# Attention heads: key norms as a product with ones over all partitions, and the inverse root as exponential of a logarithm

## The reference, cut to what matters

```python
def _rms(x, g):
    y = x * lax.rsqrt(jnp.mean(x * x, axis=-1, keepdims=True) + 1e-6)
    return y * g

k = jnp.concatenate([k_nope, jnp.broadcast_to(k_rope[:, :, None, :], ...)], axis=-1)
q, k = _rms(q, q_norm_g), _rms(k, k_norm_g)          # then rope on the last 64 channels of each
s = jnp.einsum('bhqd,bhkd->bhqk', q, k) * 192 ** -0.5
o = jnp.einsum('bhqk,bhkd->bhqd', jax.nn.softmax(s, axis=-1), v)
```

## Time and profile before

| | |
|---|---|
| median of three timed runs | 1948.47 us (1947.96 to 1952.48) |
| span of the profiled execution, first to last instruction | 1945.0 us |
| its own time | not listed apart; the median is 3.5 us above the span |
| TensorE, VectorE, ScalarE, GpSimd busy | 98%, 72%, 36%, 47% of the span |
| mean granted TensorE clock | 0.995 of full |

### The profile page before, as it was taken

One profiled execution on the slowest core, in us unless ns is written; L12 is line 12 of the kernel. 1 busy time (PEld: TensorE's weight loads), 2 busy tenths in 40 slices (PEclk: granted clock), 3 DMA queues, 4 the chain that ended last, 5 costly groups with the idle time before them and its releaser, 6 DMA issues.

```text
span 1945.0 us, 24388 instructions
## 1 busy us (share of the span) xinstructions
PE 1901.5 (98%) x9095; PEld 1580.3 (81%) x9095; DVE 1394.2 (72%) x1433; ACT 703.6 (36%) x966; POOL 909.7 (47%) x634
## 2 busy tenths in 40 slices
PE   7999999999999999999999999999999999999998
PEld 6788888778888888888888788878787878888877
DVE  7989988566449898989888774754723756666583
ACT  5433344421243333333331200342321245565543
POOL 6866666533235555555655556323133513212442
PEclk9999999999999999999999999999999999999999
DMA  5122234455112232322264434111141310000052
GB/s 167 44 63 67 87 109 141 147 163 156 44 43 87 66 97 65 97 75 86 82 242 147 146 103 168 55 33 33 33 133 52 89 37 1 12 12 1 1 173 65
DMA packets 190890, 166.42 MB, mean 86 GB/s; under 512 B 11267, under 2 KB 168912, under 8 KB 190800
## 3 DMA queue, kind: packets, MB, share of 16 engines
q1 hardware_dynamic: 189520, 162.82, 26.4%
q10 hardware_dynamic: 1280, 2.35, 0.4%
HBM read 134.73 MB, written 30.41 MB: 85 GB/s over the span
## 4 chain that ended last, share of the span: by engine, by line
PE 81%; DVE 11%; issue 3%; ACT 2%; POOL 2%; DMA 1%; SPq 0%; ACTq 0%; DVEq 0%; POOLq 0%
PE ps L953 32%; PE ps L1250 19%; PE ps L1100 15%; PE ps L1665 2%; PE ps L1483 2%; PE ps L1516 1%; PE ps L1518 1%; PE ps L1517 1%; PE ps L1497 1%; PE ps L1494 1%; PE ps L1500 1%; PE ps L1491 1%; PE ps L1503 1%; DVE win_a L2942 1%; DVE prob L2990 1%
## 5 line engine op out<-in xcount | busy, mean ns | idle before, releaser
L824 POOL TENSOR_TENSOR small<-ones 128x1 f32<-128x1 f32 x76 | 26.3, 346 | 501.4 <-PE ps L953 432.8
L953 PE MATMUL ps<-xb_hi,whi 128*128 128x512 f32 x752 | 247.2, 396 | 7.0 <-DVE xb_lo L2898 1.9
L953 PE MATMUL ps<-xb_hi,wlo 128*128 128x512 f32 x752 | 244.1, 392 | 0.0
L953 PE MATMUL ps<-xb_lo,whi 128*128 128x512 f32 x752 | 243.8, 392 | 0.0
L829 POOL TENSOR_TENSOR wlo<-raw,whi 128x1024 fp32r<-128x1024 f32 (+1 forms) x73 | 198.8, 2723 | 6.1
L869 POOL TENSOR_TENSOR wlo<-w_sums,whi 128x512 fp32r<-128x512 f32 x80 | 138.0, 1744 | 82.2 <-ACT whi L1963 82.2
L953 PEld LDWEIGHTS ps<-xb_hi,whi 128*128 128x128 f32 x752 | 141.2, 190 | 40.9 <-issue 5.7
L953 PEld LDWEIGHTS ps<-xb_lo,whi 128*128 128x128 f32 x752 | 142.1, 189 | 30.3 <-issue 0.2
L953 PEld LDWEIGHTS ps<-xb_hi,wlo 128*128 128x128 f32 x752 | 142.1, 189 | 30.2
L2367 DVE SCALAR_TENSOR_TENSOR ps<-glu_pad,tab,ps 128x1024 f32<-128x1024 f32 x116 | 149.2, 1286 | 2.9
L923 POOL TENSOR_SCALAR prob<-prob,small 128x512 f32<-128x512 f32 x64 | 50.7, 806 | 188.2 <-DVE small L2999 188.0
(11 more groups left out here) (489 smaller groups left out, 4855.8 us busy)
## 6 DMA issues: line engine op xcount, KB each, us to landing
t<-in_w_mod SPq DMA_DIRECT2D x48, 256.0 KB, 3.1
f_scratch<-t SPq DMA_DIRECT2D x22, 512.0 KB, 2.7
raw<-in_w_down SPq DMA_DIRECT2D x22, 512.0 KB, 4.4
raw<-in_w_up SPq DMA_DIRECT2D x40, 256.0 KB, 3.7
w_raw<-in_w_up SPq DMA_DIRECT2D x40, 256.0 KB, 3.6
raw<-in_w_in SPq DMA_DIRECT2D x18, 512.0 KB, 4.0
raw<-in_w_in SPq DMA_DIRECT2D x36, 256.0 KB, 3.7
w_in_raw<-in_w_in SPq DMA_DIRECT2D x32, 256.0 KB, 3.7
```

The costliest lines, as they stand in the source:

```text
L824: nc.gpsimd.tensor_tensor(small[:, 106 + slab.slot:107 + slab.slot], ones[:, 0:1], ones[:, 0:1], ALU.mult)
L953: ins = mm(dst[j], w, r[j], start=first and f, stop=last and l)
```

## The change

The rows of inverse roots are made without ever having the keys on the partitions. A matrix of ones as the weights leaves a sum over the partitions on every partition of the result. `KSQ` holds the squares of the rope channels, high halves on partitions 0 to 63 and low halves on 64 to 127 (made once, by ScalarE and VectorE), and the head's own squares go into `rkbc` itself. In each head TensorE adds both in PSUM, in three pieces of 256, 512 and 512 columns (banks 7, 5 and 6), behind `pv` and ahead of V. ScalarE reads the sums, writes the logarithm of the mean to `rkbc`, and then, in place, the exponential of -0.5 times it. A dummy activation ahead of the logarithms and one behind the exponential bring the tables for logarithm and square root.

```diff
-        def key_sums(n):
-            if n == 4:
-                pe.wait_ge(sem("lora_sq"), 4)
-                for t in range(KT):
-                    mm(PS[:, SC + 32 + t:SC + 33 + t], sqkr[:, t * P:(t + 1) * P], ones[0:ROPE, 0:1], start=True, stop=True)
...
-        gemm(j, L, XBh, XBl, KD, w8, between=key_sums)
+        gemm(j, L, XBh, XBl, KD, w8)
...
+        def key_sums(h):
+            if h == 0:
+                pe.wait_ge(sem("ksq_ready"), 2)
+            else:
+                pe.wait_ge(sem("pt_lo"), 6 * 4 * h)
+            for a, b in ((S, NKEY), (0, H), (H, S)):
+                o = PS[:, 5 * H + a:5 * H + b]
+                mm(o, onesr[:, :], KSQ[:, a:b], start=True, stop=False)
+                last = mm(o, ones[:, :], rkbc[:, a:b], start=False, stop=True)
+                if a != 0:
+                    last.then_inc(sem("ksum_pe"), 1)
...
-                query_product(h, c, 0, 0, 4 * c).then_inc(sem("nope_pe"), 1)
+                query_product(h, c, 0, 0).then_inc(sem("nope_pe"), 1)
...
             if h == 0:
                 warm(2)
+            key_sums(h)
...
+                    if i == 3:
+                        pe.wait_ge(sem("k_log"), 2 * h + 2)
...
-            key_scales(h, 0)
             pe.wait_ge(sem("q_fold"), GOES_ON["q_fold"][1] + 2 * h + 1)
+            pe.wait_ge(sem("k_log"), 2 * h + 1)
             scores(g, 0, 0, 512, 0)
-            key_scales(h, 1)
-            key_scales(h, 2)
...
+        act.wait_ge(sem("lora_sq"), 4)
+        fn(KSQ[0:ROPE, :], sqkr[:, :], ACT.Copy).then_inc(sem("ksq_hi"), 1)
...
-                fn(sqk[:, k], PS[:, k], ACT.Square).then_inc(sem("kn_sq"), 1)
+                fn(rkbc[:, k], PS[:, k], ACT.Square).then_inc(sem("kn_sq"), 1)
...
-            act.wait_ge(sem("k_var"), h + 1)
-            fn(ksd, kvar, ACT.Sqrt, scale=1.0 / QH, bias=eps_col).then_inc(sem("k_sd"), 1)
...
+            fn(sd[:, 12:13], ones[:, 0:1], ACT.Ln)
+            for n, (a, b) in enumerate(((S, NKEY), (0, S))):
+                act.wait_ge(sem("ksum_pe"), 2 * h + n + 1)
+                fn(rkbc[:, a:b], PS[:, 5 * H + a:5 * H + b], ACT.Ln, scale=1.0 / QH, bias=eps_col).then_inc(sem("k_log"), 1)
             if h % 2 == 0:
...
+                for i in range(3):
+                    value_hi(i)
+            act.wait_ge(sem("k_log"), 2 * h + 2)
+            fn(rkbc[:, :], rkbc[:, :], ACT.Exp, scale=-0.5).then_inc(sem("k_scale"), 1)
+            if h % 2 == 0:
+                for i in range(3, 5):
+                    value_hi(i)
+            fn(sd[:, 12:13], ones[:, 0:1], ACT.Sqrt)
...
-        link(nc.vector.tensor_copy(krc, PS[:, SC + 32:SC + 32 + KT]))
+        nc.vector.tensor_copy(onesr[:, :], ones[:, :]).then_inc(sem("ksq_ready"), 1)
+        dve.wait_ge(sem("ksq_hi"), 1)
+        tt(KSQ[ROPE:P, :], sqkr[:, :], f32(KSQ[0:ROPE, :]), ALU.subtract).then_inc(sem("ksq_ready"), 1)
...
-            dve.wait_ge(sem("kbc_read"), 3 * h + 3)
+            dve.wait_ge(sem("k_scale"), h + 1)
```

More of the change, by code:

```diff
@@ L284, in build_program @@
     Vl = at("v_lo", [P, KT, 2 * VD], F32R, o_xbh + 43008)
-    sqk = at("sq_head", [P, NKEY], F32, o_xbh + 53248)
+    sqk = at("sq_head", [P, S], F32, o_xbh + 53248)
     qwork = at("q_rope_work", [P, S], F32, o_xbh + 58368)
@@ L288, in build_program @@
     PTh = at("pt_hi", [P, KT, 2 * P], F32R, o_xah)
+    KSQ = at("k_rope_squares", [P, NKEY], F32R, o_t + 20480)
+    onesr = at("ones_r", [P, P], F32R, o_t + 25600)
     rkbc = at("k_scale_bc", [P, NKEY], F32, o_xah + KT * 2 * P * 4)
@@ L1432, in key_product @@
             return last
-        def key_sum(t):
-            return mm(PS[:, SC + 256 + t:SC + 257 + t], sqk[:, t * P:(t + 1) * P], ones[:, 0:1], start=True, stop=True)
+        def key_sums(h):
[9 more added lines that the diff above has]
+                    last.then_inc(sem("ksum_pe"), 1)
         def query_sum(t):
@@ L1442, in query_sum, with query_product @@
                 last.then_inc(sem("qsum_pe"), 1)
[L1444 to L1454, removed]
+        def query_product(h, c, col, at_bank):
             slot = Lin(SLABS["heads"] + h).slot
@@ L1461, in query_product @@
                 mm(o, whi[:, slot, w], CQh[:, k, q], start=k == 0, stop=False)
-                if sums is not None:
-                    key_sum(sums + 2 * k)
                 mm(o, whi[:, slot, w], CQl[:, k, q], start=False, stop=False)
-                if sums is not None:
-                    key_sum(sums + 2 * k + 1)
                 last = mm(o, wlo[:, slot, w], CQh[:, k, q], start=False, stop=k == 1)
-            if sums == 4:
-                key_sum(8)
-                key_sum(9).then_inc(sem("ksum_pe"), 1)
             return last
@@ L1716, in build_program @@
     tot = small[:, 110:126].rearrange("p (s t) -> p s t", s=2)
-    rsum4, krc, kvar, ksd = small[:, 10:14], small[:, 48:58], small[:, 66:76], small[:, 76:86]
+    rsum4 = small[:, 10:14]
     def scalar_program(act):
@@ L2191, in scalar_program, with value_hi @@
             fn(QRs[0:ROPE, :], qwork[0:ROPE, :], ACT.Copy).then_inc(sem("qr_hi"), 1)
-            act.wait_ge(sem("k_var"), h + 1)
-            fn(ksd, kvar, ACT.Sqrt, scale=1.0 / QH, bias=eps_col).then_inc(sem("k_sd"), 1)
             act.wait_ge(sem("qn_lo"), GOES_ON["qn_lo"][1] + 2 * h + 2)
             fn(sqk[:, H:S], PS[:, H:S], ACT.Square).then_inc(sem("qn_sq"), 1)
-            if h % 2 == 0:
[L2197 to L2206, removed]
+            def value_hi(i):
+                act.wait_ge(sem("v_pe"), 5 * (h // 2) + i + 1)
+                fn(Vh[:, 2 * i:2 * i + 2, :], PS[:, H * (2 + i):H * (3 + i)].rearrange("p (t n) -> p t n", t=2),
+                   ACT.Copy).then_inc(sem("v_hi"), 1)
+            fn(sd[:, 12:13], ones[:, 0:1], ACT.Ln)
+            for n, (a, b) in enumerate(((S, NKEY), (0, S))):
+                act.wait_ge(sem("ksum_pe"), 2 * h + n + 1)
+                fn(rkbc[:, a:b], PS[:, 5 * H + a:5 * H + b], ACT.Ln, scale=1.0 / QH, bias=eps_col).then_inc(sem("k_log"), 1)
+            if h % 2 == 0:
+                for i in range(3):
[6 more added lines that the diff above has]
+            fn(sd[:, 12:13], ones[:, 0:1], ACT.Sqrt)
             act.wait_ge(sem("head_var"), h + 1)
@@ L3054, in vector_program @@
                 pool_low(3)
-            dve.wait_ge(sem("ksum_pe"), h + 1)
-            tt(kvar, PS[:, SC + 256:SC + 256 + KT], krc, ALU.add).then_inc(sem("k_var"), 1)
             query_lo(1)
@@ L3060, in vector_program @@
             query_fold(0)
-            dve.wait_ge(sem("k_sd"), h + 1)
-            nc.vector.reciprocal(rcp[:, 0:KT], ksd).then_inc(sem("k_rcp"), 1)
             if h:
```

## The result

The changed kernel takes 1954.47 us, the median of 13 runs (1950.87 to 1956.68), against 1948.52 for the kernel before (13 runs, 1945.47 to 1952.48). The ratio is 1.0028, 95% interval 1.0021 to 1.0036: 4 to 7 us slower, at the edge of what is called no change here. 1951.4 was forecast, with 1945.0 to 1955.5 as its range. The profiled execution has a span of 1953.3, 8.3 more than before.

What follows compares the result with a forecast made beforehand. TensorE, busy in 98% of the span, was taken as the bound. The terms -2.4 - 1.65 + 0.6 + 1.4 + 1.7 + 3.3 = +2.95 us on about 1948.5 gave 1951.4 us, range 1945 to 1955.5.

Steps and rivals of the forecast that it cites:

- Part two: Heads 1 to 3: removing ten key sums gains 0; pv still waits for VectorE's rope query, gap 0.45 to 2.75 us.
- faster rival: Heads 1 to 3: the rotated query comes earlier, 2.3 us won in each, no gaps: 1941.2 us, chance 0.08.
- Parts three and four: New sums cost 3.1 us per head, +0.85 each odd head; logarithm chain +0.6 in head 0, +1.4 in head 2.
- The reserve: Odd heads: ScalarE's logarithms, loads and exponential end 0.65 us before the query's square root wants ScalarE.
- slower rival: ScalarE becomes the bound through table changes in the heads, 7.7 us more: 1959, chance 0.16.
- part one: Ahead of the heads: removing the rope keys' ten one-column sums gains 2.4 us, their low-clock stretch 1.65 more.
- Part five: Low clock behind the gaps in heads 1 to 3: chance 0.6 each, 1.65 us lost each, two likeliest, +3.3.
- hit every time: All three gaps in heads 1 to 3 are followed by a low-clock stretch: 1953.1 us, chance 0.14.
- the cases: Number of gaps followed by low clock: none or one 0.20, two 0.42, all 0.14; 1948.2 to 1953.1 us.
- The base: Kernel before: about 1948.5 us, profiled span 1945.0 plus 3.5 us taken as lying around the span.

Runs made afterwards that it cites:

- two_more_loads: The changed kernel with a dummy logarithm and a dummy root more in heads 1 and 3, so two table loads more in each: 1958.85 us, ratio 1.0043.
- wide_fill3: The changed kernel with three warming products of 512 columns, read by nobody, filling the whole gap ahead of pv in heads 1 to 3: 1950.48 us.
- sums_in_gap: The changed kernel with the new key sums moved from behind pv into the gap ahead of it in heads 1 to 3: 1940.74 us, ratio 0.9966.
- ga_sums_back: The changed kernel with the ten one-column products on the rope keys' squares back in the first ga projection, read by nobody: 1955.22 us.
- narrow_fill: The changed kernel with ten one-column products, read by nobody, in the gap ahead of pv in heads 1 to 3: 1954.03 us.
- wide_fill: The changed kernel with two warming products of 512 columns, read by nobody, in the gap ahead of pv in heads 1 to 3: 1954.10 us.

## Why the prediction was right, and where it was not

The measured time lies in the range, and parts two to four held in their mechanism. But the change is 6.0 us by the medians where 2.95 was forecast: the clock cost more than forecast in both of its terms, in parts one and five.

*Part two held.* VectorE's rope query stays where it was, and the removed sums became wait. Its first step and the one that `pv` waits for, in head 3 of the changed kernel:

```profile
1789.14 1.23 DVE L3035 TENSOR_TENSOR q_rope_work<-ps,cos_sin_q 64x1024 f32<-64x1024 f32 x1 [0.55 <-ACT q_rope_work L2159]
...
1792.80 1.21 DVE L3042 TENSOR_TENSOR q_rope_work<-ps,q_rope_work 64x1024 f32<-64x1024 f32 x1
```

`pv` starts 4.92 us behind the first step, as before (1785.14 to 1790.05, 4.91). The gap is 2.56 where 2.75 was forecast. The faster rival falls with it.

*Parts three and four held, each a little dear.* The sums take 1798.98 to 1801.31 and 0.4 for the slower first product behind, 2.7 us instead of 3.1. Without the longer `pv`, head 3 lost 0.6 us from `pv` to the scores row (5.8 - 4.0 - 1.25), against 0.85, and head 1 lost 0.4. The even heads came close: head 0 lost 0.5 (from -1.2 to -0.7 in the table) against 0.6, and head 2 lost 1.3 (2.8 - 1.5) against 1.4. ScalarE in head 3:

```profile
1801.91 1.12 ACT L2187 ACTIVATE k_scale_bc<-ps,small 128x1024 f32<-128x1024 f32 x1 [1.71 <-PE ps L1438]
1803.04 1.28 ACT L2192 ACT_TABLE_LOAD   x1
1804.34 1.27 ACT L2192 ACTIVATE k_scale_bc<-k_scale_bc 128x1280 f32<-128x1280 f32 x1
1805.63 1.28 ACT L2196 ACT_TABLE_LOAD   x1
...
1807.46 0.21 ACT L2198 ACTIVATE small<-small 128x8 f32<-128x8 f32 x1 [0.34 <-DVE small L3065]
```

The logarithm at 1.1 and the exponential at 1.27 are as taken, and each load is followed within 0.02 us. The reserve is 0.34 us, half of the forecast's 0.65, and it holds. So the slower rival did not come. The drain of 1.38 us that the Trainium skill gives (ScalarE: Activation LUTs, What ACT_TABLE_LOAD costs) shows in neither kernel, and two_more_loads, which would have lost about 10 us by it, lost 4.4. In head 0 the wait for the logarithm is 2.4 (2.25 was forecast), and the one for the fold follows, as worked out; the wait for `v_lo`, 2.0 before, is still there with 0.8. In head 2 TensorE waits for the fold (0.8) and not for the logarithm, as said.

*The step that failed is the clock's in part one.* "Both the sums and this stretch go" is wrong in its second half: the sums went (2.4 us in the trace), the stretch stands behind the next block of one-column products. Of the nine traces, the two with both blocks have one stretch there, behind the first; of the seven with one block, six have one behind it. Removing a block saved its time and no stretch, so the term of -1.65 was 0.

*Part five was mis-sized.* Three gaps of three were followed by 0.50, not two: the rival "hit every time". `pv` took 5.17, 5.16 and 4.92 us where 3.67 is its price, so a stretch there cost 1.25 to 1.5 and not 1.65, 4.2 in all instead of 3.3. Over all traces, `pv` behind a gap of 2.56 left open or a block of one-column products has 0.50 in 12 cases of 12, and behind a filled one (the kernel before among them) in none of 15. In the 12 `pv` took 4.92 to 5.18 us, in the 15 it took 3.63 to 3.69. The chance of 0.6 each was far too low. Nor do the chances of the cases follow from it: 0.6 each makes 0.27 for none or one, 0.33 for two and 0.16 for all three out of 0.76, and not 0.20, 0.42 and 0.14.

With these two terms set right (+1.65, +0.9) and the sums at their measured price (-0.8 over two odd heads, at 0.4 each), the forecast's 1951.4 becomes 1953.2, 1.3 below the median. The rest is not settled. Part of it can be low stretches elsewhere: the mean granted clock is 0.9908 over the 13 runs of the changed kernel and 0.9943 over the 41 of the kernel before. Lines of one common slope, one line for the runs of each kernel (113 in all), give 1.4 us for each 0.001 of clock, so 4.9 us for these 0.0034 or so, and at one clock the two kernels lie within 0.4 us of each other. That is a correlation, which wide_fill3 and sums_in_gap support for the three gaps only.

*The base was right as a median, not for the reason given.* The forecast took 3.5 us to lie around the span. In the runs that have both numbers 1.7 to 1.9 us lie around it, so the profiled execution of the kernel before took about 1946.8 (an estimate, 1945.0 and 1.8) and was one of its faster ones.

*So the profiled 8.3 us hold more than the median.* 1.2 arose ahead of the change, where the clock fell at other places. Behind the heads the wait for `out_copies` is longer, before and after:

```profile
PE ps L1665 <- DVE out_copies L3144: 1.1, 1, 1.1
```

```profile
PE ps L1647 <- DVE out_copies L3132: 3.3, 1, 3.3
```

The long wait stands in three traces of nine (the changed kernel and both wide fills), the very three whose stretch of 0.50 near the end lies at 1898 to 1902, behind this wait, and not between 1849 and 1879. In the six others the stretch falls in the products ahead of the wait, makes TensorE come later to it, and is hidden there: 1.1 us of wait are left. Behind the wait it lies open, 1.6 of the 2.5 us. The other 1.0 is VectorE's: from TensorE's wait for `xa_lo` to the end of this one 32.1 us pass in the six traces and 33.2 in the three. Which of VectorE's steps is slower differs among the three, and why was not tested. Three kernels with the whole change (ga_sums_back, narrow_fill, two_more_loads) are among the six, so the change alone does not bring this; whether it makes it more frequent, nine traces do not tell.

## What to carry to other kernels

Work taken from an engine that waits right behind it for another becomes a gap. Here the gap cost twice, in time not won and in a low clock behind it, so try to put the other half of the change into it: moving the new sums there turned 6 us lost into 7 to 8 us won. As filler, real work or products of 512 columns kept the clock here; a block of one-column products, counted as busy, did not. Where one of several like lulls goes, look at the next one before booking its low-clock stretch as a gain.

## What was not expected

- Ten one-column products (2.29 us busy, 0.44 waiting) were followed by the low clock as surely as 2.56 us of waiting: 3 of 3.
- The same program has from 1944.85 us at a mean clock of 0.997 to 1954.60 at 0.992 (wide_fill), so differences of a few us need many runs or the rows of the place itself.
